# A PEER value table: half of its columns streamed whole through TensorE for two of three token tiles, the other half gathered

## The reference

```
q = (h2 @ peer_wq)                         # 8 heads x 2 x 128
s1, i1 = top_k(scores with keys 1, 16); s2, i2 = top_k(scores with keys 2, 16)
sc, j = top_k(all 256 sums s1 + s2, 16); eid = i1 * 128 + i2 of those 16
g = softmax(sc)
a = gelu(einsum('td,thkd->thk', h2, peer_u[eid]))
y = x1 + gate2 * einsum('thk,thkd->td', g * a, peer_v[eid])
```

## Time and profile before

| | |
|---|---|
| time, median of 3 runs | 2571.34 us (2564.22 to 2575.87) |
| the profiled execution, first to last instruction | 2572.8 us |
| busy PE / PEld | 1280.7 (50%) / 697.2 (27%) |
| busy DVE | 1757.6 (68%) |
| busy ACT / POOL | 212.5 (8%) / 1184.3 (46%) |
| DMA | 944.49 MB, mean 367 GB/s |
| gathers' queue (q0) | 682.66 MB, 66.0% of the 16 engines' span |
| SP's queue (q1) | 260.74 MB, 28.2% |

### The profile page before, as it was taken

How to read it: one execution, slowest core, us unless ns; L and a number is a source line. 1 busy time by engine, 2 the same in 40 slices (tenths; PEclk the granted TensorE clock), 3 DMA queues, 4 the chain that set the end, 5 groups by cost and what they waited for, 6 DMA issues and landing times.

```text
span 2572.8 us, 17754 instructions
## 1 busy us (share of the span) xinstructions
PE 1280.7 (50%) x6315; PEld 697.2 (27%) x6317; DVE 1757.6 (68%) x2243; ACT 212.5 (8%) x559; POOL 1184.3 (46%) x686
## 2 busy tenths in 40 slices
PE   5699998897490543266884972000015655200000
PEld 2363534482240432143331960000002222000000
DVE  1010112217967977897557667999999998899898
ACT  3110012100001221121001010000000000000000
POOL 1000100002426744575222415678876767788684
PEclk9799898899795655556995985555556677655555
DMA  9949899659999999999998989999999999999897
GB/s 299 332 172 422 324 414 291 208 196 360 388 422 397 377 366 341 405 410 370 344 373 321 414 318 410 366 393 422 422 407 407 400 420 417 417 422 422 366 422 307
DMA packets 163042, 944.49 MB, mean 367 GB/s; under 512 B 34635, under 2 KB 44435, under 8 KB 56830
## 3 DMA queue, kind: packets, MB, share of 16 engines
q0 software_dynamic: 94784, 682.66, 66.0%
q1 hardware_dynamic: 68175, 260.74, 28.2%
HBM read 937.36 MB, written 10.26 MB: 368 GB/s over the span
## 4 chain that ended last, share of the span: by engine, by line
PE 27%; DMA 25%; DVE 20%; POOL 15%; issue 9%; SPq 2%; ACT 1%; POOLq 0%; another core or an unknown queue 0%; DVEq 0%; ACTq 0%
POOL arena L668 11%; DMA arena<-in_peer_u,arena 10%; DMA arena<-in_peer_v,arena 9%; DVE arena L1975 8%; POOL arena L680 4%; DVE arena L1998 4%; DMA arena<-in_w_out 4%; PE PS L1468 3%; PE PS L1445 3%; PE PS L1016 3%; DMA arena<-in_w_ada 3%; PE PS L1166 2%; PE PS L1253 2%; PE PS L966 2%; PE PS L1423 2%
## 5 line engine op out<-in xcount | busy, mean ns | idle before, releaser
L668 POOL DMA_INDIRECT arena<-in_peer_u,arena x256 | 471.7, 1843 | 446.1 <-DVE arena L1975 240.8
L1975 DVE CUSTOM_DVE_ANT_0 arena<-arena 128x2048 f32<-128x2048 f32 x256 | 581.5, 2289 | 118.0 <-DMA arena<-in_peer_u,arena 116.7
L1998 DVE SCALAR_TENSOR_TENSOR arena<-arena 128x2048 f32<-128x2048 f32 x226 | 531.1, 2350 | 136.6 <-DMA arena<-in_peer_v,arena 131.9
L668 POOL DMA_INDIRECT arena<-in_peer_v,arena x256 | 428.3, 1673 | 369.7 <-DVE arena L1998 242.7
L1468 PE MATMUL PS<-arena 128*128 128x512 f32 x240 | 180.3, 921 | 449.9 <-DMA arena<-in_peer_v,arena 449.9
L1468 PEld LDWEIGHTS PS<-arena 128*128 128x128 f32 x240 | 69.5, 304 | 561.4 <-issue 555.1
L1474 PE MATMUL PS<-arena 128*64 128x512 f32 x8 | 5.5, 849 | 346.4 <-DVEq L2041 346.4
L2031 DVE SCALAR_TENSOR_TENSOR arena<-arena 128x2048 f32<-128x2048 f32 x64 | 150.6, 2352 | 10.8 <-DMA arena<-in_peer_v,arena 5.3
L966 PE MATMUL PS<-arena 128*32 128x512 f32 x768 | 119.4, 721 | 69.9 <-DMA arena<-in_w_ada 66.6
L2028 DVE CUSTOM_DVE_ANT_0 arena<-arena 128x2048 f32<-128x2048 f32 x64 | 145.0, 2291 | 8.4 <-DMA arena<-in_peer_u,arena 6.5
L680 POOL DMA_INDIRECT arena<-in_peer_v,arena x64 | 126.4, 1975 | 39.0 <-issue 18.6
(11 more groups left out here) (347 smaller groups left out, 1824.5 us busy)
## 6 DMA issues: line engine op xcount, KB each, us to landing
arena<-in_w_ada SPq DMA_DIRECT2D x96, 1024.0 KB, 12.1
arena<-in_w_in SPq DMA_DIRECT2D x32, 1048.0 KB, 9.2
arena<-in_peer_wq SPq DMA_DIRECT2D x32, 1024.0 KB, 10.2
arena<-in_w_in SPq DMA_DIRECT2D x32, 768.0 KB, 11.2
arena<-in_w_out SPq DMA_DIRECT2D x16, 1024.0 KB, 30.0
arena<-in_w_out SPq DMA_DIRECT2D x32, 512.0 KB, 24.0
arena<-in_peer_u,arena POOLq DMA_INDIRECT x320, 13.9
arena<-in_peer_v,arena POOLq DMA_INDIRECT x320, 15.5
```

Source lines behind the costliest of these rows:

```text
L668: pool.indirect_dma_start(out=rows_ring[:, k % NROW, :], out_offset=None, in_=tables[kind], in_offset=bass.IndirectOffsetOnAxis(ap=ids[:, ...
L1975: V.tensor_tensor_reduce(out=buf, in0=buf, in1=h2(t), scale=1.0, scalar=0.0, op0=ALU.mult, op1=ALU.add, accum_out=dots[:, t, r:r + 1]).the ...
L1998: V.scalar_tensor_tensor(out=acc[t], in0=rows_ring[:, k % NROW, :], scalar=dots[:, t, r:r + 1], in1=acc[t], op0=ALU.mult, op1=ALU.add).the ...
```

## The change

- peer_v's columns are split. For tiles 0 and 1, phase v gathers only columns 0 to 1023 (128 x 4 KB a gather, from the table seen as 32768 half rows, with doubled ids eid2). The accumulators have 1024 columns.
- Columns 1024 to 2047 are streamed whole: 128 blocks of 128 table rows x 1024 columns (0.5 MB) by SP into four buffers, and multiplied on TensorE by expert weight matrices WT[t] (for each block, 128 experts x 128 tokens), four 128x512 matmuls a block, accumulated in four PSUM banks.
- WT[t] is made from one-hot matrices: for a token, hot2 (its 128 experts by key 2) times hot1 (by key 1, weighted) is a 128x128 matmul. 32 groups of 4 tokens a tile. DVE makes hot1, and half of hot2 for tile 1; ACT makes the other hot2 and empties PSUM into WT.
- The order of phases is now u0, v0, u1, u2, v1, v2. experts(2, ...) move from v1 to u1, where the one-hots of tile 0 follow; those of tile 1 are made beside u2. Block 0 is loaded at once, block 1 when u1's dots are done, the others when both WT are nearly made.
- v1's rows on TensorE (PE_ROWS) are gone, and the loops of the last two phases are written out. Row buffers are twelve cells of 4 KB, a whole row takes two; v1 has eight cells, v2 four whole rows.
- Five of the eight sample steps move from v0 into u0; pauses are Q 4, K 4, OUT 14, WQ 36.
- On ACT the exponential of the second half of tile 0's experts moves behind the copies and the root that it stood ahead of; gelu(0) moves behind the fifth sample step.
- x1 of tiles 1 and 2 is parked in DRAM too, and all three are read back at the end. finish(0) and finish(1) run after all rows.

```diff
-NROW = 6
-N_INLINE = 4
-Q_PAUSE, K_PAUSE, S_PAUSE, OUT_PAUSE, WQ_PAUSE = 12, 20, 3, 20, 30
-LOOP_ROW0 = N_INLINE * 128 - NROW
+GC = 1024
+DC = D - GC
+N_BLK = 128
+N_VD = 4
+N_GRP = 32
+HOT_ACT = (4, 2)
+N_EARLY_B = 5
+Q_PAUSE, K_PAUSE, S_PAUSE, OUT_PAUSE, WQ_PAUSE = 4, 4, 3, 14, 36
...
+        R_W0, R_W1, R_FREE = 30784, 8192, 30784 + N_BLK * 128
+        WT = [view(R_W0, N_BLK, 128), view(R_W1, N_BLK, 128)]
+        idsf = view(R_FREE, 2, 128)
+        eid2 = [view(12288, PH, TOPK).bitcast(I32), view(R_FREE + 256, PH, TOPK).bitcast(I32)]
...
+        rows_of_slot = [view(D * i, D) for i in range(6)]
+        acc0 = view(R_H2, GC)
...
-        PHASES = [("u", 0), ("v", 0), ("u", 1), ("v", 1), ("u", 2), ("v", 2)]
+        PHASES = [("u", 0), ("v", 0), ("u", 1), ("u", 2), ("v", 1), ("v", 2)]
...
             load(n_in1 + 2, n_wq1)
...
+            for i in range(N_BLK):
+                if i == 1:
+                    sp.wait_ge(s_dots, 2)
+                if i == 2:
+                    sp.wait_ge(s_wmm, 2 * N_GRP)
+                wait(sp, s_vused, i - N_VD + 1)
+                sp.dma_start(vd[i % N_VD], I["peer_v"][rows_of(i), GC:D]).then_inc(s_vin[i % N_VD], 16)
...
+            sp.wait_ge(s_vused, N_BLK)
+            sp.dma_start(XB[0], parked).then_inc(s_backx[0], 16)
+            sp.dma_start(XB12, parked12).then_inc(s_backx[1], 16)
             for t in range(2):
                 sp.wait_ge(s_y, t + 1)
-                sp.dma_start(O["y_prompt"][0, t * 128:(t + 1) * 128, :], acc[t]).then_inc(s_yst[min(t, 1)], 16)
...
+            half_rows = I["peer_v"].rearrange("n (a d) -> (n a) d", a=D // GC)
+            for kind, t in PHASES:
...
+                    if is_half(kind, t):
+                        table, ids = half_rows, eid2[t].rearrange("p a b -> p (a b)")
+                    else:
+                        table = I["peer_u"] if kind == "u" else I["peer_v"]
+                        ids = eid[:, t].rearrange("p a b -> p (a b)") if t < 2 else eid_s
+                    wait(pool, s_rowfree, row_former[k] + 1)
+                    pool.indirect_dma_start(out=row_buffer(kind, t, k), out_offset=None, in_=table,
+                                            in_offset=bass.IndirectOffsetOnAxis(ap=ids[:, r:r + 1], axis=0)).then_inc(s_row[row_cell[k]], 16)
...
-            def expert_exp(t):
-                for half in range(2):
-                    w = gw[:, t, half * HH:(half + 1) * HH]
-                    act.wait_ge(s_e2, 2 * t + half + 1)
-                    A(w, w, exp).then_inc(s_e2x, 1)
+            def expert_exp(t, half):
+                w = gw[:, t, half * HH:(half + 1) * HH]
+                act.wait_ge(s_e2, 2 * t + half + 1)
+                A(w, w, exp).then_inc(s_e2x, 1)
...
-            expert_exp(0)
+            expert_exp(0, 0)
...
+            expert_exp(0, 1)
...
-            gelu(0)
...
+                if b == N_EARLY_B - 1:
+                    gelu(0)
...
-            expert_exp(1)
+            expert_exp(1, 0)
+            expert_exp(1, 1)
+            expert_exp(2, 0)
+            expert_exp(2, 1)
...
+            def one_hot(t, g):
+                n = N_GRP * t + g
+                wait(act, s_wmm, n - 1)
+                for j in range(HOT_ACT[t]):
+                    token = 4 * g + j
+                    last = A(hot2[:, g % 2, j, :], iota128, ACT.Abs, bias=i2N[:, token:token + 1], scale=1.0)
+                last.then_inc(s_abs, 1)
+                act.wait_ge(s_abs, n + 1)
+                v = hot2[:, g % 2, 0:HOT_ACT[t], :]
+                A(v, v, ACT.Relu, bias=ones_col, scale=-1.0).then_inc(s_hot2, 1)
+            def expert_weights(t):
+                ids_out(t)
+                one_hot(t, 0)
+                for g in range(N_GRP):
+                    if g + 1 < N_GRP:
+                        one_hot(t, g + 1)
+                    act.wait_ge(s_wmm, N_GRP * t + g + 1)
+                    A(WT[t][:, :, 4 * g:4 * g + 4], PS[:, 4 + g % 2, :].rearrange("p (t i) -> p i t", t=4), copy).then_inc(s_wev, 1)
+            act.wait_ge(s_parkx12, N_CST + 16)
+            expert_weights(0)
             gelu(1)
-            expert_exp(2)
...
+            expert_weights(1)
+            gelu(2)
+            act.wait_ge(s_vused, N_BLK)
+            for t in range(2):
+                A(YD[t], PS[:, 2 * t:2 * t + 2, :].rearrange("p a b -> p (a b)"), copy).then_inc(s_yd, 1)
...
+            def expert_weights(t):
+                pe.wait_ge(s_ids, N_CPS + t + 1)
+                turn(PS[:, 7, 0:128], idsf[:, 0, :], ident)
+                turn(PS[:, 7, 128:256], idsf[:, 1, :], ident)
+                turn(PS[:, 7, 256:384], dots[:, t, :], ident).then_inc(s_idp, 1)
+                for g in range(N_GRP):
+                    n = N_GRP * t + g
+                    pe.wait_ge(s_hot1, n + 1)
+                    pe.wait_ge(s_hot2, n + 1)
+                    wait(pe, s_wev, n - 1)
+                    for j in range(4):
+                        last = mm(PS[:, 4 + g % 2, j * 128:(j + 1) * 128], hot2[:, g % 2, j, :], hot1[:, g % 2, j, :], start=True, stop=True)
+                    last.then_inc(s_wmm, 1)
+            expert_weights(0)
+            expert_weights(1)
+            pe.wait_ge(s_wev, 2 * N_GRP)
+            for i in range(N_BLK):
+                pe.wait_ge(s_vin[i % N_VD], VIN_BASE[i % N_VD] + 16 * (i // N_VD + 1))
+                for t in range(2):
+                    for n in range(2):
+                        last = mm(PS[:, 2 * t + n, :], WT[t][:, i, :], vd[i % N_VD][:, n * SECTION:(n + 1) * SECTION], start=(i == 0), stop=(i == N_BLK - 1))
+                last.then_inc(s_vused, 1)
...
-            for j, k in enumerate(PE_ROWS):
-                pe.wait_ge(s_diag, j + 1)
-                pe.wait_ge(s_row[k % NROW], 16 * (k // NROW + 1))
-                for n in range(4):
-                    last = mm(PS[:, n, :], diag[:, j % 2, :], rows_ring[:, k % NROW, n * SECTION:(n + 1) * SECTION],
-                              start=(j == 0), stop=(j == len(PE_ROWS) - 1))
...
+                for b in range(N_EARLY_B):
+                    yield from sample_step(b, 2)
+            def sample_step(b, n):
+                yield from pause(n)
+                smp_norm(b)
+                if b + 1 < DB:
+                    yield from pause(n)
+                    s_max(b + 1)
+                yield from pause(n)
...
+                for b in range(N_EARLY_B, DB):
+                    yield from sample_step(b, 3)
...
+            def ids(t):
+                idi = idsf.bitcast(U32)
+                wait(dve, s_idT, t)
+                V.tensor_scalar(idi[:, 0], eid_u[:, t], 7, None, ALU.logical_shift_right)
+                link(V.tensor_scalar(idi[:, 1], eid_u[:, t], 127, None, ALU.bitwise_and))
+                V.tensor_copy(idsf, idi).then_inc(s_ids, 1)
+            def one_hots(t):
+                for g in range(N_GRP):
+                    if g == 0:
+                        dve.wait_ge(s_idT, t + 1)
+                    wait(dve, s_wmm, N_GRP * t + g - 1)
+                    for j in range(HOT_ACT[t], 4):
+                        token = 4 * g + j
+                        V.tensor_scalar(hot2[:, g % 2, j, :], iota128, i2T[:, token:token + 1], None, ALU.is_equal)
+                    for j in range(4):
+                        token = 4 * g + j
+                        last = V.tensor_scalar(hot1[:, g % 2, j, :], iota128, i1T[:, token:token + 1], wT[:, token:token + 1], ALU.is_equal, ALU.mult)
+                    last.then_inc(s_hot1, 1)
+                    yield
             def beside_dots1():
-                yield from paced(experts(1, 1), 2)
+                yield from experts(1, 1)
                 yield from pause(2)
                 shares(1)
-            def beside_sums1():
-                yield
-                dve.wait_ge(s_g2, 8)
-                dve.wait_ge(s_backx, 16)
-                finish(0)
-                yield
-                for half in range(2):
-                    yield from paced(experts(2, half), 2)
+                yield from experts(2, 0)
+                yield from experts(2, 1)
                 yield from pause(2)
                 shares(2)
                 sample_experts()
...
-            def weights(t):
+                yield
+                ids(0)
+                yield from pause(2)
+                yield from one_hots(0)
+            def beside_dots2():
+                yield from pause(2)
+                yield from one_hots(1)
...
-            def sum_rows(t, k0, beside):
...
+            def sum_rows(t, total, beside):
...
+                    V.scalar_tensor_tensor(out=total, in0=row_buffer("v", t, k), scalar=dots[:, t, r:r + 1], in1=total, op0=ALU.mult, op1=ALU.add).then_inc(s_rowfree, 1)
+                    dve.wait_ge(s_rowfree, k + 1)
...
+            def finish(t):
+                gate = PS[:, 4:8, :].rearrange("p a b -> p (a b)")
+                dve.wait_ge(s_g2p, 1)
+                dve.wait_ge(s_yd, N_SIG + t + 1)
```

(19 more changed lines are left out.)

288 lines of the change are left out of this document (126 added, 162 removed).

## The result

The changed kernel took 2624.34 us (median of 4 runs, 2615.7 to 2634.8) against 2571.20 us for the kernel before (4 runs): a ratio of 1.0216, 95% interval 1.0191 to 1.0240. It is slower by 53 us, some 2%; 2530 was forecast, with 2612 as the upper end of the range. Both levels need an explanation. The profiled execution of the changed kernel spans 2617.3 us, that of e9 2589.4 us.

A forecast was written before the change was run, and what follows sets the result against it. Gathers bound by bytes, with a chain ahead of u1: u1 starts 122 us sooner at 1442, VectorE-bound one-hots last to 1959, 229 MB take 553 us to 2512, plus a 19.3 us tail: 2531, median 2530; range 2485 to 2612.

The forecast's parts named there:

- 9. end: After the last sum: eight 128x1024 operations make the tail 19.3 us in place of 15.3, ending at 2531 us.
- Steps 1 to 5: Attention, w_out, norm, peer_wq, experts(1,0): the chain ahead of u1 shortens, so u1 starts at 1442 us, 122 us sooner.
- five stated cases: Rivals: stream ends last 13%, chain unmoved 13%, POOL misses VectorE's gaps 9%, half-size DMAs slower 5%, more gained 8%.
- step 4: peer_wq and scores: TensorE at full clock, unchanged at 99 us, scores at 1376 us.
- step 1: Up to the samples' attention's end: early sample steps, moved exponential and shorter pauses end it near 1110 us, 85 us sooner.
- step 5: experts(1,0): 22 half rows between its pieces make it 55 us in place of 28, done at 1431 us.
- Steps 6 and 7: u1 and u2 to the last one-hot group: VectorE-bound, 398 us (62 longer), then 115 us, reaching 1959 us.
- rival C: GpSimd misses VectorE's gaps between half rows: v1 307 us in place of 250, experts(1,0) 26 longer, end 2587; 9%.
- Step 8: From the last one-hot group to the last row: 229 MB at 413 GB/s, 553 us, to 2512 us.
- A: The stream ends last, TensorE waiting at each block or at the lower clock; typically 2600 to 2700 us; 13%.
- B: The chain ahead of u1 hardly moves, attention gaining 30 us in place of 85 while u1 gets longer; 2585 us; 13%.
- D: Half-size DMAs in v1 and the stream move at 349 GB/s in place of 413: 59 us, end 2590; 5%.

The follow-up runs named there:

- e9: The changed kernel measured again, unaltered, on another chip; 2592.59 us, ratio 1.0084 to the kernel before.
- e16: The changed kernel with all eight sample steps back in v0 (N_EARLY_B = 0); 2616.66 us, one run.
- e18: The changed kernel with the exponential of tile 0's second half of experts back ahead of ScalarE's copies; 2622.21 us, one run.
- e1: The changed kernel with WQ_PAUSE 36 -> 68, putting v0's last 32 half rows ahead of experts(1,0); 2622.37 us, ratio 1.0212.
- e6: e1's kernel with 4 cells in place of 12 for v0's half rows; 2627.72 us, ratio 1.0218.
- e8: The changed kernel with stream blocks from the fifth on loading only 256 of their 1024 columns; 2488.08 us, one run.
- e11: The changed kernel with six cells in v0 and nothing else changed; 2606.64 us, ratio 1.0109.
- e5: e1's kernel with 6 cells in place of 12 for v0's half rows; 2587.90 us, ratio 1.0059.
- e7: The changed kernel with two of four matmuls per stream block left out, except first and last block; 2589.89 us, one run.
- e2: The changed kernel with ScalarE making all of tile 1's second one-hots; 2611.10 us, ratio 1.0166.
- e13: The changed kernel with the edits of e1 and e2 together, on a chip without gaps; 2553.51 us, ratio 0.9915.
- e15: e10's kernel with most of VectorE's one-hots left out; 2494.68 us, one run.
- e4: The kernel before with only the change's order of steps: whole rows, no stream, no one-hots; 2550.16 us, ratio 0.9927.
- e14: e13's kernel with tile 1's one-hot groups after every second row of u2; 2549.50 us, ratio 0.9899.
- e17: e14's kernel with WQ_PAUSE 62 and the last six half rows behind an uninterrupted experts(1,0); 2616.57 us, ratio 1.0179.
- e10: e1's kernel measured again on another chip, beside e9; 2566.53 us, ratio 0.9976.

## Why the prediction was wrong

Its steps against the two executions of the changed kernel:

| | forecast | recorded | e9 |
|---|---|---|---|
| 1. samples' last copy | 1110 | 1122 | 1107 |
| 2. w_out done | 1235 | 1252 | 1237 |
| 3. first peer_wq matmul | 1277 | 1298 | 1283 |
| 4. scores there | 1376 | 1413 | 1381 |
| 5. experts(1,0) done | 1431 | 1469 | 1437 |
| u1 starts | 1442 | 1483 | 1451 |
| 6, 7. last one-hot group | 1959 | 2023 | 1991 |
| 8. last row | 2512 | 2598 | 2570 |
| 9. end | 2531 | 2617 | 2589 |

**Steps 1 to 5 hold in e9**, to 6 us at most. The recorded execution loses 15 us in the attention and 17 in peer_wq, where its gaps are; 28 us of it are left at the end. Without them the time would have lain inside the range (e9, 2593), but still on the other side of the kernel before than forecast. Nothing in the profile of before shows such gaps, and none of the five stated cases has them. The prediction took it as certain that peer_wq beside half-row gathers runs as it did beside whole rows (step 4, "unchanged, 99 us": 98 in e9, 115 recorded). In step 1 the early sample steps carry the gain (65 us, e16); the moved exponential hardly any of it (e18), though I had reckoned with 45 us of it: the wait moved to VectorE. That the step came out within 3 us in e9 all the same is in part luck.

**Between step 5 and u1** I counted 22 half rows beside experts(1,0) and overlooked ten more behind it, 13 us that took the place of the first gather's 11: only a few us, since one covers the other.

**Steps 6 and 7 were mis-sized, by 23 us** (540 in place of 517). I priced a one-hot at 0.2 us from L1993, which has one operation in it. The weighted one-hot compares and multiplies, with two operands per partition. The row of the changed kernel:

```profile
1985.12 0.47 DVE L2062 TENSOR_SCALAR arena<-arena 128x128 f32<-128x128 f32 x2
1985.52 1.10 DVE L2065 TENSOR_SCALAR arena<-arena 128x128 f32<-128x128 f32 x4
1986.54 2.27 DVE L2102 CUSTOM_DVE_ANT_0 arena<-arena 128x2048 f32<-128x2048 f32 x1
```
Two plain ones take 0.40 us, four weighted ones 1.02: 0.255 each. That is 14 us over 64 groups. Most of the other 9 is the gather of 11.8 us shown above. Eleven profiles have the change's one-hots in full, and they tell its price: with such a gather in u1 (the recorded execution, e1, e6, e8 to e11) the stretch takes 539 to 543 us, without it (e5, e7, e16, e18) 531 to 534, though e7's program differs from e9's only in the stream, which comes later. That is some 8 us. By the look of the trace it is rival C's mechanism, POOL kept from issuing by a VectorE that doesn't pause, in a phase where I had not looked for it; no run tests it by itself. Whether it happens differs from run to run. The last rows of u1, which ran at the DMA's 2.49 us while I had put all at VectorE's 2.21, and the 7 us from u1's last row to u2's first in place of 4 add a few us; other terms came out a little smaller.

The mechanism of steps 6 and 7 stands: what was taken from VectorE here came off the end nearly one for one (e2, e13, e15). It is also what makes the change lose: 54 us of moved experts (by the forecast's 27 each) and 78 us of one-hots (32 groups of 1.02 us and 32 of 1.42) keep the DMA at 317 GB/s for 540 us.

**Step 8 was mis-sized, by 26 us** (579 in place of 553). The bytes were right (229 MB forecast, 402 GB/s x 578 us = 232 MB) and so was the bound (e7, e8); the rate was not. With both queues full it is 409 to 413, but phase v2 with its four whole-row buffers in place of eight moved 374 GB/s from 2500 to 2568 us in e9 (412 before), and the first 60 us, while the stream starts, 373. The same holds behind the stream in every profile, up to 5 us ahead of the last row: with four buffers 376 to 399 GB/s (386 in e9) and in e11 344, with eight 422 (the kernel before from 2400 us, e4 from 2375). POOL waited there for VectorE to free a buffer, 17.5 us in all in e9, where it was 4.4 in the kernel before. No run changed the buffers of v2 alone, so their part is argued from these waits. The front of this document shows the four buffers; I gave them no price. By my estimate from these rates, of the 26 us some 7 are the 3 MB more, 6 the first 60 us, 8 the end of v2, and 4 the 409 in place of 413 between.

**The rivals.** A (stream last, or TensorE at its lower clock): no; a block took 3.57 us against 3.46 forecast, at a granted clock of 1.00. (The forecast's 2415 for its end should have been 1959 + 443 = 2402; nothing hangs on it.) The Trainium skill (TensorE: Matmul & The Clock Gate, section HAM oscillation) warns of a loop that falls to the low clock at every wait for a tile, and its waits are longer than its computing. The stream never came near that: TensorE waited 1.7 us for blocks in all, and even in e7, with 27.5 us of waits in 120, none over 1.0 us, the clock stayed at 1.00. So no run here tests the page's case. B (the chain ahead of u1 doesn't move): no, it moved 113 us in e9 and 81 in the recorded execution, where what held it back were the gaps and not the attention's own pace. C (POOL misses VectorE's gaps): not where I had put it, v0's half rows ran at 1.31 us from start to start; but the same mechanism cost some 8 us in u1. D (half-size DMAs slower): no, blocks and gathers of 0.5 MB moved 409 GB/s together. The Trainium skill (DMA: Bandwidth & Descriptors, section Bandwidth) wants at least 1 MiB a transfer for 75% of peak; with several in flight this case doesn't bear it out. None of the rivals was "VectorE cannot feed the DMA in u1 and u2 for longer than reckoned", which is where most of the time went; it stood in the sum with no margin. Both mis-sized steps lay on the path and erred to the same side (49 us), and the range had been cut from rivals and not from them. In short: the one-hots' price, a gather that POOL could not issue in time, and v2's rate failed by 49 us, while the bytes and the bound held; the gaps, whose cause is open, took the recorded execution 28 us further, out of the range.

## What to carry to other kernels

Bytes saved in one phase are worth what the phases that must now prepare the saving leave unfilled: here 63 MB less (881.9 against 944.5) are 153 us of DMA time at 410 GB/s. They were saved ahead of u1, where a chain and not the bytes set the time, so that u1 came only 81 us sooner; and preparing the stream left 121 us of DMA idle behind it. Work that moves to VectorE beside gathers is free only up to the difference between the engine's row and the DMA's row, 0.28 us here. Try the reordering by itself as well: it gave 0.7% (e4) without any of the new machinery, nearly as much as the whole change after three mends (1.0%, e14). And measure on more than one chip before a per cent is believed: e17, which is e14 with one small edit more, was 1.8% slower than the kernel before on the next chip, and e4 itself ran on one only.

## What the runs showed of the hardware

- TensorE can stand between matmuls with nothing in the profile to wait for: one matmul of 0.48 us every 2.8 us, 34 us of waits in peer_wq (e1). It was so in the recorded execution and on two of the five chips of the study, only while POOL issued 4 KB-row gathers one every 1.3 us, and it ended 1 to 5 us after the last of them though the DMA stayed full (415 GB/s). It was not so under whole rows (e4, same chip and call), nor in v1, where half-row gathers came one in 2 us: the stream's 1024 matmul records took 456 us in e1 as in e9. The same kernel was 56 us apart between two chips (e1, e10). What holds the matmuls back is open. POOL's row of issues can be a cause or a result, since in e10, without gaps, the peer_wq loads took their share and POOL kept that pace for 38 us only; a smaller pile of gathers could not be tested on a chip with the gaps; and chip and placement in memory can't be told apart.
- A gather's issue on POOL can take 11.8 us when it begins under a row of VectorE's 128x2048 dots without a pause (five of them, 11.1 us); it ended 0.8 us after the last. Among one-hots each took 2.9 us.
- Two queues fill the DMA as well as one: 409 GB/s (e7, the recorded execution), shared by packets (6757 and 6724 in e7; 523 and 527 with 3.84 and 2.03 MB). With four buffers of 1 MB whole rows came at 376 to 399 GB/s, with eight at 422; six of 0.5 MB for half rows beside other loads cost 14 us (e11).
- A one-hot with two per-partition operands costs VectorE 0.255 us from start to start at 128x128, one with one operand 0.20.
